# Seven norms by halves of the tokens: the product ahead, the fill and the next product's first unit

## The reference

```
h = h + dsa_attention(rms_norm(h, g_attn_a)) ; h = h + sq_relu_mlp(rms_norm(h, g_mlp0))
k, v, f = split(rms_norm(h, g_kv) @ w_kv)
h = h + fox_attention(rms_norm(h, g_attn_b)) ; h = h + sq_relu_mlp(rms_norm(h, g_mlp1))
x = rms_norm(h, g_final)
x = x + g1 * gqa_attention(modulate(rmsnorm(x, n1), sh1, sc1)) ; x = x + g2 * mlp(modulate(rmsnorm(x, n2), sh2, sc2))
x = x + g1 * chunked_gmlp(modulate(rmsnorm(x, n1), sh1, sc1)) ; x = x + g2 * mlp(modulate(rmsnorm(x, n2), sh2, sc2))
```

## Time and profile before

| what | value |
|---|---|
| median of 3 runs | 2616.79 us (2616.62 to 2617.0) |
| the profiled execution, and its span | 2616.5 us, 2615.2 us |
| mean granted clock of TensorE | 0.99 |
| busy: PE, DVE, POOL, ACT | 98%, 50%, 48%, 37% |
| chain that ended last | PE 86%, DVE 8%, ACT 2%, issue 2% |

### The profile page before, as it was taken

The page is one execution under the profiler, slowest core; times in us unless marked ns, Lnnn a source line. Parts: engine busy times, 40 slices in busy tenths (PEclk is TensorE's granted clock), DMA queues, the critical chain, the costliest instruction groups (busy, mean ns, idle before and its releaser), DMA issues.

```text
span 2615.2 us, 33003 instructions
## 1 busy us (share of the span) xinstructions
PE 2558.4 (98%) x13362; PEld 2070.2 (79%) x13362; DVE 1295.5 (50%) x2151; ACT 979.9 (37%) x1620; POOL 1245.9 (48%) x618
## 2 busy tenths in 40 slices
PE   8989999999999999999999999999999999999999
PEld 5667788887776788888777788887888888788887
DVE  4873899842036499992686432122335223432121
ACT  4474423223347342232467432232324223432231
POOL 4864444444457454444577344443443444444442
PEclk9999999999999999999999999999999999999999
DMA  4102555532220365542210233332422222233332
GB/s 146 58 24 66 184 191 179 185 114 73 97 81 2 114 192 193 193 161 97 101 61 18 82 97 97 100 100 101 141 81 81 97 97 81 81 97 97 100 99 77
DMA packets 260891, 277.03 MB, mean 106 GB/s; under 512 B 7172, under 2 KB 249476, under 8 KB 260484
## 3 DMA queue, kind: packets, MB, share of 16 engines
q1 hardware_dynamic: 259140, 272.31, 32.2%
q10 hardware_dynamic: 1600, 2.62, 0.3%
HBM read 270.19 MB, written 2.10 MB: 104 GB/s over the span
## 4 chain that ended last, share of the span: by engine, by line
PE 86%; DVE 8%; ACT 2%; issue 2%; POOL 1%; DMA 0%; SPq 0%; ACTq 0%; DVEq 0%
PE bank L463 22%; PE bank L464 22%; PE bank L465 22%; DVE acc L1409 3%; PE bank L641 2%; PE bank L531 2%; PE bank L532 2%; PE bank L533 2%; PE bank L596 2%; DVE tmp L1444 2%; PE bank L439 2%; PE bank L440 2%; PE bank L443 2%; PE bank L624 1%; DVE Hlo L1447 1%
## 5 line engine op out<-in xcount | busy, mean ns | idle before, releaser
L1753 POOL TENSOR_TENSOR wlo<-raw,whi 128x1024 fp32r<-128x1024 f32 (+1 forms) x408 | 987.7, 2442 | 1204.2 <-ACT whi L923 1204.1
L463 PE MATMUL bank<-Xhi,whi 128*128 128x512 f32 (+1 forms) x1616 | 639.3, 396 | 1.4 <-POOL wlo L1753 1.4
L464 PE MATMUL bank<-Xlo,whi 128*128 128x512 f32 (+1 forms) x1616 | 630.3, 390 | 0.0
L465 PE MATMUL bank<-Xhi,wlo 128*128 128x512 f32 (+1 forms) x1616 | 629.4, 389 | 0.0
L923 ACT ACTIVATE whi<-raw 128x1024 fp32r<-128x1024 f32 (+1 forms) x408 | 404.9, 1041 | 575.9 <-PE bank L465 496.0
L463 PE MATMUL bank<-Hhi,whi 128*128 128x512 f32 x1024 | 400.8, 391 | 0.0
L464 PE MATMUL bank<-Hlo,whi 128*128 128x512 f32 x1024 | 399.1, 390 | 0.0
L465 PE MATMUL bank<-Hhi,wlo 128*128 128x512 f32 x1024 | 398.6, 389 | 0.0
L463 PEld LDWEIGHTS bank<-Xhi,whi 128*128 128x128 f32 (+1 forms) x1616 | 302.3, 187 | 72.0 <-issue 6.6
L465 PEld LDWEIGHTS bank<-Xhi,wlo 128*128 128x128 f32 (+1 forms) x1616 | 302.4, 187 | 65.7
L464 PEld LDWEIGHTS bank<-Xlo,whi 128*128 128x128 f32 (+1 forms) x1616 | 302.5, 187 | 63.4 <-issue 1.7
(11 more groups left out here) (271 smaller groups left out, 3114.1 us busy)
## 6 DMA issues: line engine op xcount, KB each, us to landing
ada<-in_ada_w SPq DMA_DIRECT2D x48, 1024.0 KB, 5.2
raw<-in_w_up SPq DMA_DIRECT2D x32, 1024.0 KB, 5.7
raw<-in_w_down SPq DMA_DIRECT2D x32, 1024.0 KB, 5.0
raw<-in_mlp_w_in SPq DMA_DIRECT2D x32, 1024.0 KB, 5.6
raw<-in_mlp_w_out SPq DMA_DIRECT2D x32, 1024.0 KB, 5.0
raw<-in_gmlp_w_in SPq DMA_DIRECT2D x24, 1024.0 KB, 5.0
raw<-in_gmlp_w_out SPq DMA_DIRECT2D x12, 1024.0 KB, 5.1
raw<-in_w_in_a SPq DMA_DIRECT2D x8, 1024.0 KB, 5.2
```

Source lines behind the costliest of these rows:

```text
L463: pe.matmul(b[0:rows, :], whi[s][:, c, j:j + rows], hi[:, c, :], start=(c == 0), stop=False)
L464: pe.matmul(b[0:rows, :], whi[s][:, c, j:j + rows], lo[:, c, :], start=False, stop=False)
L465: m = pe.matmul(b[0:rows, :], wlo[s][:, c, j:j + rows], hi[:, c, :], start=False, stop=(c == KC - 1))
L1753: pool.tensor_tensor(wlo[u % 2][:, c0:c1, 0:k], src[:, c0:c1, 0:k], whi[u % 2][:, c0:c1, 0:k].bitcast(F32), ALU.subtract).then_inc(lo_done, 1)
```

## The change

For the seven seams (the new table HALVED gives each fill its event):

- The last unit of the product ahead runs by halves of the tokens (`last`): first tokens 0 to 255 of both tiles in their own banks, then tokens 256 to 511 in banks 4 and 5. Each matmul has 256 moving tokens. The first half's mean (`norm_means`) stands behind c = 4 of the second half's first tile, its transposes (`norm_rows`) behind that tile.
- DVE and ACT take the last two chunks by halves (`add_half`, `square_half`, `add_square_half`).
- The fill (`seam`, in place of recip, wait_rows, root and fill) has 16 parts of 256 tokens: 8 chunks of the first half, then 8 of the second (in g in another order), with the second half's norm, and ACT's split of unit u + 1, between parts of the first half. In the fills of SHARED GpSimd makes Xlo of parts 1, 3, 11, 13 and 15, elsewhere none, and it splits unit u + 1 behind parts 1 and 3. `ahead=1` in `units` leaves that split out where it stood.
- The next product's first unit (`halved`) takes the first half's parts for both tiles, then the second half's; the second half's mean stands behind c = 3 of the first half, its transposes behind c = 5. In `tm_wide` (gv) the tokens are the stationary side: token blocks 0 and 1, then 2 and 3, with 512 columns moving as before, and mean and transposes behind c = 1 and c = 2; c runs to 3 in that unit, and the next unit takes the other chunks.
- The rows of m1 now go to banks 6 and 7, as the others; the rows kept for the fill of qb are copied by halves.

```diff
+HALVED = {"m0": "oa", "kv": "m0", "m1": "ob", "c": "m1", "m2": "oc", "g": "m2", "m3": "go"}
+def fill_order(f):
+    if f == "g":
+        return [0, 1, 2, 3, 4, 5, 8, 9, 10, 11, 6, 7, 12, 13, 14, 15]
+    return list(range(2 * KC if f in HALVED else KC))
+def pool_lows(f):
+    return () if f not in SHARED else (1, 3, 11, 13, 15) if f in HALVED else (1, 4, 7)
+def high_parts(f, k):
+    return fill_base(f)[0] + fill_order(f).index(k) + 1
...
+        def norm_means(e, h, both):
+            pe_until.wait_ge(sum_half, square_base(e)[2] + 2 * both * (h + 1))
+            for k, total in enumerate((rstd, gained)[:both]):
+                for i in range(2):
+                    m = pe.matmul(bank[6 + h][:, 2 * k + i:2 * k + i + 1], total[:, (2 * h + i) * P:(2 * h + i + 1) * P], mean[:], start=True, stop=True)
+            m.then_inc(ms_full, 1)
+        def norm_rows(e, h):
+            pe_until.wait_ge(ms_recip, 2 * EVENTS.index(e) + h + 2)
+            if e == "m1":
+                pe_until.wait_ge(z_root, h + 1)
+            to_rows(bank[6 + h], rcol[:, NT:2 * NT], rows_full, (2 * h, 2 * h + 1))
...
+            if halved:
+                s, e = gm.unit % 2, HALVED[halved]
+                for j in range(2):
+                    wait_bank(gm.tile + j)
+                for h in range(2):
+                    for c in range(KC):
+                        if h == 0 and c % 4 == 0:
+                            wait_unit_half(gm.unit, c // 4)
+                        wait_high(halved, KC * h + c)
+                        for j in range(2):
+                            b = bank[(gm.tile + j) % 4]
+                            pe.matmul(b[:, tokens(h)], whi[s][:, c, j * P:(j + 1) * P], hi[:, c, tokens(h)], start=(c == 0), stop=False)
+                            pe.matmul(b[:, tokens(h)], wlo[s][:, c, j * P:(j + 1) * P], hi[:, c, tokens(h)], start=False, stop=False)
+                        wait_part(halved, KC * h + c)
+                        for j in range(2):
+                            m = pe.matmul(bank[(gm.tile + j) % 4][:, tokens(h)], whi[s][:, c, j * P:(j + 1) * P], lo[:, c, tokens(h)], start=False, stop=(c == KC - 1))
+                            if h and c == KC - 1:
+                                m.then_inc(tile_done, 1)
+                        if h == 0 and c == 3:
+                            norm_means(e, 1, 1 + (e == "m1"))
+                        if h == 0 and c == 5:
+                            norm_rows(e, 1)
...
+            if last:
+                u = gm.unit + len(gm.widths) - 1
+                s = u % 2
+                for h in range(2):
+                    for j in range(2):
+                        g = gm.tile + o + j
+                        b = bank[4 + j if h else g % 4]
+                        if h == 0:
+                            wait_bank(g)
+                        for c in range(KC):
+                            if h == 0 and j == 0 and c % 4 == 0:
+                                wait_unit_half(u, c // 4)
+                            pe.matmul(b[:, tokens(h)], whi[s][:, c, j * P:(j + 1) * P], hi[:, c, tokens(h)], start=(c == 0), stop=False)
+                            pe.matmul(b[:, tokens(h)], whi[s][:, c, j * P:(j + 1) * P], lo[:, c, tokens(h)], start=False, stop=False)
+                            m = pe.matmul(b[:, tokens(h)], wlo[s][:, c, j * P:(j + 1) * P], hi[:, c, tokens(h)], start=False, stop=(c == KC - 1))
+                            if h and j == 0 and c == 4:
+                                norm_means(last, 0, 1 + (last == "m1"))
+                        m.then_inc(tile_done if h else part_done, 1)
+                        if h and j == 0:
+                            norm_rows(last, 0)
...
-        def norm_rows(e, gain=False):
-            done, added = square_base(e)
-            n, both = EVENTS.index(e), 1 + gain
-            pe_until.wait_ge(sq_add, added + (KC - 2) * both)
-            for k, total in enumerate((rstd, gained)[:both]):
-                for i in range(NT):
-                    pe.matmul(bank[6 + i // 2][:, 2 * k + i % 2:2 * k + i % 2 + 1], total[:, i * P:(i + 1) * P], mean[:],
-                              start=(k == 0 and i % 2 == 0), stop=False, skip_group_check=True)
-            for h in range(2):
-                if h:
-                    pe_until.wait_ge(sq_done, done + KC * both)
-                else:
-                    pe_until.wait_ge(sq_half, half_base(e) + both)
-                for k in range(both):
-                    last = held[(both * (KC - 2) + k) % 3]
-                    for i in (2 * h, 2 * h + 1):
-                        m = pe.matmul(bank[6 + h][:, 2 * k + i % 2:2 * k + i % 2 + 1], last[:, i * P:(i + 1) * P], mean[:],
-                                      start=False, stop=(k == both - 1 and i % 2 == 1), skip_group_check=True)
-                m.then_inc(ms_full, 1)
-            for h in range(2):
-                pe_until.wait_ge(ms_recip, 2 * n + h + 2)
-                to_rows(bank[4 if gain else 6], rcol[:, NT:2 * NT], rows_full, (2 * h, 2 * h + 1))
...
+        def seam(e, name, f, shift, gain=None):
+            g, u = GEMM[name].end - 2, GEMM[name].unit + len(GEMM[name].widths)
+            act.activation(warm[:], eps[:, 0:1], ACT_F.Sqrt)
+            square_half(e, g, KC - 2, 0, gain)
+            square_half(e, g + 1, KC - 1, 0, gain)
+            root(e, 0)
+            square_half(e, g, KC - 2, 1, gain)
+            for p, k in enumerate(fill_order(f)):
+                h, c = k // KC, k % KC
+                act_until.wait_ge(xq_done, xq_base(f) + p + 1)
+                if h:
+                    act_until.wait_ge(tile_done, GEMM[name].end)
+                else:
+                    act_until.wait_ge(part_done, 2 * EVENTS.index(e) + 2)
                 if shift is None:
-                    act.activation(Xhi[:, c, :], tmp[c % 4][:], ACT_F.Copy).then_inc(x_hi, 1)
+                    act.activation(Xhi[:, c, tokens(h)], tmp[c % 4][:, tokens(h)], ACT_F.Copy).then_inc(x_hi, 1)
                 else:
-                    act.activation(Xhi[:, c, :], tmp[c % 4][:], ACT_F.Identity, bias=shift[:, c:c + 1]).then_inc(x_hi, 1)
-        def square(e, g, c, gain=None):
-            done, added = square_base(e)
-            both = 1 if gain is None else 2
-            if c == KC - 2:
-                act.activation(warm[:], eps[:, 0:1], ACT_F.Sqrt)
-            for h in range(1 + (c == KC - 1)):
-                at = slice(256 * h, 256 * h + 256) if c == KC - 1 else slice(0, S)
-                if c == KC - 1 and h == 0:
-                    act_until.wait_ge(half_set, EVENTS.index(e) + 1)
-                else:
-                    act_until.wait_ge(*freed(g))
-                for k, total in enumerate((rstd, gained)[:both]):
-                    n = both * (c - 1) + k
-                    q = total if c == 0 else held[n % 3]
-                    if n >= 3:
-                        act_until.wait_ge(sq_add, added + n - 2)
-                    a = act.activation(q[:, at], HT[:, c, at], ACT_F.Square, scale=1.0 if k == 0 else gain[:, c:c + 1])
-                    a.then_inc(sq_half if c == KC - 1 and h == 0 else sq_done, 1)
-        def root(e, gain=False):
-            n = EVENTS.index(e)
-            for h in range(2):
-                act_until.wait_ge(ms_full, 2 * n + h + 1)
-                act.activation(rcol[:, 2 * h:2 * h + 2], bank[6 + h][:, 2 * gain:2 * gain + 2], ACT_F.Sqrt, bias=eps[:, gain:gain + 1]).then_inc(ms_root, 1)
-            for h in range(2 * gain):
-                act.activation(zcol[:, 2 * h:2 * h + 2], bank[6 + h][:, 0:2], ACT_F.Sqrt, bias=eps[:, 0:1]).then_inc(z_root, 1)
+                    act.activation(Xhi[:, c, tokens(h)], tmp[c % 4][:, tokens(h)], ACT_F.Identity, bias=shift[:, c:c + 1]).then_inc(x_hi, 1)
+                if p == 3:
+                    square_half(e, g + 1, KC - 1, 1, gain)
+                    split(u + 1, (0,))
+                if p == 5:
+                    root(e, 1)
+                if p == 6:
+                    split(u + 1, (1,))
...
+        def seam(e, name, f, gain, shift, gate=None, both=1):
+            g, n, order = GEMM[name].end - 2, EVENTS.index(e), fill_order(f)
+            for c in (KC - 2, KC - 1):
+                add_half(e, g + c - KC + 2, c, 0, gate)
+                add_square_half(e, c, 0, both)
+            recip(e, 0)
+            add_half(e, g, KC - 2, 1, gate)
+            def low(k):
+                if k in pool_lows(f):
+                    return
+                h, c = k // KC, k % KC
+                q, hi, lo = tmp[c % 4][:, tokens(h)], Xhi[:, c, tokens(h)].bitcast(F32), Xlo[:, c, tokens(h)]
+                dve_until.wait_ge(x_hi, high_parts(f, k))
+                if shift is None:
+                    dve.tensor_tensor(lo, q, hi, ALU.subtract).then_inc(x_lo, 1)
+                else:
+                    dve.scalar_tensor_tensor(lo, q, shift[:, c:c + 1], hi, ALU.add, ALU.subtract).then_inc(x_lo, 1)
```

(40 more changed lines are left out.)

362 lines of the change are left out of this document (199 added, 163 removed).

## The result

The changed kernel takes 2633.57 us, median of 4 runs (2631.69 to 2636.43), where the kernel before took 2616.89 in the same rounds (2616.62 to 2617.21): a ratio of 1.0064, 95% interval 1.0052 to 1.0077. It is 16.7 us slower. I had forecast 2613.9, range 2600 to 2624. The profiled execution has a span of 2632.2 us, 17.0 more than before.

The account below looks back on a forecast made before the run. TensorE, busy 98% of the span, was taken as the bound. Of 51.5 us lost in seven seams the added work takes 17 and waits bring back some 31, leaving 3 us gained: 2613.9 us, range 2600 to 2624.

Parts of the forecast that it names:

- The first gap: TensorE's stop between last unit and next product, 4.75 us in m0 to kv; claimed gone with the change.
- narrow matmuls: Halved units need more matmuls, each over 256 tokens at 0.120 us: 0.64 us more a unit, 8.3 us in all.
- VectorE is held by GpSimd: VectorE instructions with two SBUF tensors wait until GpSimd's ends, 2.4 us for half a weight unit; PSUM operands escape.
- PE pays at parts 4 and 6: In the next product's first unit TensorE waits for Xlo 4 and 6, walked 1.24 and 1.69 us.
- the walk: Step-by-step timing of one seam over the engines: 28.34 us, all seven 200.9 against 203.9; as walked, chance 0.46.
- g 26.85 (...) its first unit has only four parts in each half, but waits 0.9 for tile 7's bank.: Seam m2 to g: walked 26.85 us against 29.15 before.
- my rivals: Collisions missed or short, faster, 0.34; clock falls all the same, slower, 0.17; halves don't start early, 0.03.
- add, square 3.94, sum held by GpSimd to 5.3: no harm: First half of tile 6 in the last unit: add and square done at 3.94, the held sum costs nothing.
- I charge 0.31 us for each such pair: Norm's means and transposes inside the stream: 1.24 us a seam, 0.44 more for m1, 9.1 us in all.
- Eight one-column matmuls take 0.95 us: Reading of the old norm's matmuls in the trace, 0.11 us apart, used to price the new norm.
- a fall in five seams or more: Half clock after the seams' waits, 1.7 us each; decides from five seams, all seven +12, 2626; chance 0.17.
- c alone, nothing that decides: Half clock in two or three seams, or only in c with its 2.7 us wait, wouldn't decide the outcome.

Follow-up runs that it names:

- e4: Kernel before, with 13 weight units outside the seams taken over 256 tokens at a time, nothing else of the change: 2620.75 us, ratio 1.0014.
- e11: Changed kernel, load of gv's second weight unit issued ahead of the two broadcasts but still behind the wait for m2d3's end: 2629.01 us, ratio 1.0048.
- e1: Changed kernel, load of gv's second weight unit issued ahead of the two broadcasts and of the wait for m2d3's end: 2624.85 us, ratio 1.0025.
- e10: Changed kernel with e6's new order and finer GpSimd splits, but without the early load and early table load: 2606.62 us, ratio 0.9955.
- e2: e1 plus a tiny early square root on ScalarE in oa, ob, oc and go, moving the table load out of the seam: 2619.27 us, ratio 1.0004.
- e9: e6 with each of the norm's one-column mean matmuls issued twice: 2599.79 us.
- e6: e2 with an instruction order of its own and GpSimd's wlo of the first two units behind each norm in eight instructions each: 2593.32 us, ratio 0.9909.
- e5: e2 with the seam's same instructions in another, walked order, GpSimd's split still in two instructions: 2606.01 us, ratio 0.9957.

## Why the prediction was wrong

**What held.** The first gap goes in every seam (none is left of the earlier trace rows's waits for Xhi); narrow matmuls are 0.120 apart (e4); VectorE is held by GpSimd where two of its inputs are in SBUF (its products, with one input in PSUM, took 0.48 us at most, all 112 of them), and PE pays at parts 4 and 6, most in m1 to c (2.4 at its means, walked 2.7). Where nothing else came in, m0 to kv, the walk gave 28.34 for 28.36, and not by luck: counted from start to start, PE's four stops cost 0.44, 1.12, 1.95 and 0.50 us, where the walk had 0.48, 1.32, 1.77 and 0.49 with the restarts (the profile's brackets, 0.17, 0.86, 1.69 and 0.24, leave part of each stop out).

**The step that failed: "g 26.85 (...) its first unit has only four parts in each half, but waits 0.9 for tile 7's bank."** It measured 36.04. The 0.9 was right (1.05), but I had moved ScalarE's weight split forward in the walk, behind part 3, and never asked whether its weights were there. They are loaded by SyncE, and at this one place SyncE first waits for the end of m2d3 and issues two broadcasts (e11: 2.7 and 6.0 us of the seam). Before, there were 12.5 us between issue and use; the change left none, and root, reciprocal and rows of the second half queue behind that split. Cost 8.7 us (e1), and 12.0 in the seam of e10. Of the 19.7 us between forecast and result this is the largest single part, and it was none of my rivals.

**A cover that was gone: ScalarE's table load.** The walk has ScalarE free for the square at 3.94 ("add, square 3.94, sum held by GpSimd to 5.3: no harm"). In four seams a table load of 1.28 us stands there. It cost 5.6 us by the medians (e2, uncertain by some 2), 4.3 by the waits. The Trainium skill, "ScalarE: Activation LUTs", section "What ACT_TABLE_LOAD costs", gives about 1283 ns, and the row has 1.28; the price was to be had, what I had missed is that a load hidden before was no longer hidden.

**A term wrong in its parts: "I charge 0.31 us for each such pair".** "Eight one-column matmuls take 0.95 us" misread: "x8" were four matmuls of the program, each with two records. A pair of means costs 0.44 us with the way back into wide matmuls, not 0.31 (e9's rows). But a pair of transposes costs only 0.22 (m0 to kv: the next two matmuls start 0.14 and 0.08 late), so a seam pays 1.32 us and not 1.24, and over all seven seams the term is short by only about 1 us. Here two slips do cancel, by luck.

**The clock.** I gave a fall in five seams or more a chance, and "c alone, nothing that decides". It fell in three, one of them only because of the wait in g. Of the sum's 18.2 us over the walk at most 8 are half clock, and probably less, since at half clock PE needs VectorE's parts later. In m1 to c the changed kernel had two stretches (10.2 us, waits at Xlo of 0.8 and 0.8) and took 34.45, e2 had one of 3.4 us and waited more (up to 1.8 at once): 33.52. What decides whether a given seam falls isn't settled: with nearly the same waits m0 to kv kept full clock in all runs, and oa to m0 lost it in e2 but not in the changed kernel. Nor does the row hold that I had set against a fall, the wait of 2.4 us for TC, a tile of attention c, behind which the clock kept 1.00: in the changed kernel the same wait, 2.4 us up to 1351.23, has half clock at its end (1350.80 to 1354.20, above).

**The range.** Its upper end, 2624, came from the clock alone. In the sum no seam came out clearly shorter than walked: here a walk over four engines left things out, and what it left out was waiting each time.

**Was the idea wrong?** No: e6 is the same change, with one load, the table loads, the orders and the length of GpSimd's instructions mended, and is 0.9% faster than before. The largest single part of what it wins back, 13 us (e5), is the order: VectorE stood in front of the root and the rows of the second half with the Xlo that PE wanted next right behind.

## What to carry to other kernels

When a step is moved forward on an engine, follow back what it reads to the queue that fetches it, and look at what else that queue has just been given: the wait is not that step's alone but that of all behind it in order. List what was hidden at the old place (table loads, broadcasts, a long instruction of GpSimd) and price each uncovered. And when halving makes a chain finer, put short instructions of VectorE and GpSimd in it and choose the order by a walk over all engines: here the halved seams lost 17 us in the first order, gained 12 in a walked order with shorter instructions of GpSimd (e10), and 24 with the load ahead as well (e6).
